# One inference step with 96 attention units and a paged decode: the order of the work of one unit step on TensorE

## The chip, the cores and the metric

The kernel runs on one core of one Trainium2 chip. The metric is the device time of one launch in microseconds (us), the median of several runs. Everything is computed in float32.

## What is computed

One layer of a hybrid decoder, for a prompt of 512 tokens and for 8 decode sequences of one new token each with 4096 cached tokens. Two attention branches run side by side: sparse attention (compressed, selected and sliding window keys) and latent attention (MLA). Both are gated, projected and added to the input:

```python
p_w = _masked_softmax(s_w, mask_w)                         # sliding window; the selected branch alike
o_w = einsum('bqgrs,bsgd->bqgrd', p_w, kvw[..., 1, :])
s = (einsum('bqhc,bsc->bhqs', q_lat, c) + einsum('bqhr,bsr->bhqs', q_pe, kr)) * MLA_SCALE   # c, kr: paged caches
o_lat = einsum('bqhs,bsc->bqhc', _masked_softmax(s, mask), c)
pa = (o_a * silu(ga)) @ w_proj_a
pb = (o_b * silu(gb)) @ w_proj_b
h = sigmoid(ma) * pa + sigmoid(mb) * pb                    # ga, gb, ma, mb = xn @ w_in (gate columns)
y = x + rmsnorm(h @ w_out, norm_post)
```

The page table says which pages of the caches belong to which sequence, so the latent cache (256 pages of 128 tokens, kept with its transpose, 256 KB a page) is loaded page by page.

## The kernel before

The kernel is written by hand for the five engines, each with its own instruction stream; they meet in semaphores. It has a first part (projection, compression and selection), a loop of 99 unit steps, and a tail (merge of the decode parts, the output projections, the norm). The change lies in the loop and in TensorE's stream alone.

**The loop.** Step u = 0..98 puts up to four streams of work beside each other on TensorE:

- *The prompt's units.* 96 units, each one head and one block of 128 queries against 128 to 512 keys. `scores(u)` (L889) runs on even u and writes the scores of units u and u+1 into two PSUM banks; it waits until ScalarE has taken the exponentials (L1236) of units u-2 and u-1. `transposes(u-2)` (L897) turns the probabilities; it waits until VectorE has scaled them and until the transposes of the unit before are copied out. `outputs` (L910) on even u multiplies units u-4 and u-3 with the values, after both copies.
- *The decode's chunks.* 80 steps from u = 2 on: `K` steps turn keys (`dec_keys`, L932), `C` steps treat one chunk c. `dec_scores(c)` (L950) needs the chunk's data in its ring slot, and waits until the exponentials of the chunk before it are taken (they free bank 5). VectorE then forms the maximum (L1775), ScalarE the exponential (L1253). One step later `dec_transposes(c)` (L920) turns the probabilities, VectorE or ScalarE copies them out, and `dec_outputs(c)` (L961) multiplies them with the values. Its last matmul raises `do_ps`.
- *The fills.* From u = 36 to 95 each step has a quarter of one column block of the gate projection, in four parts, `fill(u, 0)` to `fill(u, 3)`. Steps come in fives (x = 0..4): for x < 4 a part is one 128x512 gate product (L980), for x = 4 (u = 40, 45, 50, ..., 95) it is eight small products for the decode rows (L985). Bank 3 has to be read out after x = 1, 3 and 4, and the next fill waits for that reading (L1299 on ScalarE, L1291 and L1832 for the silu gates).

**The order in the other streams.** VectorE takes in a step: silu of the last fill, the copy of `dec_transposes` (every other chunk), `unit_max(u)` (L1728), the maximum of the chunk, the scaling of unit u-1, the copy of unit u-2, the reading of `outputs`, and `dec_fold` after `dec_outputs`. ScalarE takes: the reading of the last fill, its share of the copies, the exponentials of unit u, then those of the chunk, then its share of the unit copies. All are strictly in order, so a copy that waits holds up what is queued behind it.

**The MLA chunks and their loads.** Steps 42 to 81 hold eight groups of five: for each sequence a chunk "new" (the new token, no load) and four parts, each with its own load of 2 MB into a ring of three slots. The part steps of the first group are u = 43, 44, 45, 46, of the second 48, 49, 50, 51, and so on: the fourth part always meets x = 0, and the step before it x = 4. SyncE starts the eight page loads (L500) of job n as soon as the slot's last user, the chunk three loads earlier, has raised `do_ps`:

```python
            elif J_WIN <= m < J_WV:
                eng.wait_ge(S["do_ps"], last_chunk[m] + 1)        # slot_free, m = n - RING, RING = 3
```

The fourth part's slot is that of the first part of the same sequence, whose `dec_outputs` is in the step after its `dec_scores`. GpSimd fetches the rotary keys of the job (L537) after the same signal.

**The array's shapes.** The products use TensorE's array in four shapes: whole (128x128: `transposes`, `dec_transposes`, `dec_keys`, the L980 fills, and `scores` of the units 0 to 31 with 96 rows), four column strips (128x32: `dec_scores`, `dec_outputs`, the L985 fills), two column strips (128x64: `outputs`), and 64 rows (`scores` from unit 32 on).

Of the kernel before, what the change touches and what calls it, by code (L numbers as in the profile page):

```python
# [167 lines left out]
def build(nc, t):  # L168

    ctx = ExitStack()  # L170
    with ctx:
# [34 lines left out]
        def C(name, lo=0, width=None, rows=P):  # L206
            off, _, w = CST[name]
            return cst[0:rows, off + lo:off + (w if width is None else lo + width)]
# [111 lines left out]
        def job_landed(eng, n):  # L320

            eng.wait_ge(S[slot_sem(n)], landed[n])
# [3 lines left out]
        chunks = []  # L326
# [20 lines left out]
        UNITS = 96  # L347
# [16 lines left out]
        def dt_copied(eng, m):  # L364

            if m >= 0:
                eng.wait_ge(S["dt_by_" + dt_use[m]], sum(1 for e in dt_use[:m + 1] if e == dt_use[m]))
# [16 lines left out]
        def fill_free(eng, ev):  # L384

            if ev >= 0:
                def silu(e):
                    return FILL_JOBS[e // 3][0] in ("ga", "gb")
                eng.wait_ge(S["fill_by_dve" if silu(ev) else "fill_by_act"], sum(1 for e in range(ev + 1) if silu(e) == silu(ev)))
# [40 lines left out]
        def unit(u):  # L430

            if u < 32:
                return 2, 2 * (u // 8) + u % 2, (u % 8) // 2
            v = u - 32
            return (v % 4) // 2, 2 * (v // 16) + v % 2, (v % 16) // 4
# [7 lines left out]
        def pt_by(u):  # L443
            return "A" if u % 2 else "V"
# [141 lines left out]
        def K_of(c):  # L586
            r, part = c["r"], c["part"]
            out = []
            for j in range(4):
                if c["kind"] == "win":  # L590
                    q = QZw[:, (4 * r + j) * 32:(4 * r + j + 1) * 32]
                    out.append([(q, KnW if part == "new" else KTs[:, j * 512:(j + 1) * 512], 0, c["width"])])
                elif c["kind"] == "slc":
                    s2 = 0 if part == "new" else part
                    q = QZs[:, ((4 * r + j) * 2 + s2) * 32:((4 * r + j) * 2 + s2 + 1) * 32]
                    out.append([(q, KnS[:, (j % 2) * 8:(j % 2) * 8 + 8] if part == "new" else KTs[:, j * 512:(j + 1) * 512], 0, c["width"])])
                else:
                    ql = [QL[:, (ck * 8 + r) * 32:(ck * 8 + r + 1) * 32] for ck in range(2)]
                    qr = [QR[:, (r * 4 + v) * 32:(r * 4 + v + 1) * 32] for v in range(4)]
                    if part == "new":  # L600
                        out.append([(ql[0], cTn[:, 0:8], 0, 8), (ql[1], cTn[:, 8:16], 0, 8), (qr[0], krn, 0, 8)])
                    else:
                        pages = job(c["job"]).rearrange("p (q c) -> p q c", q=8)
                        kr = KRR[:, ((c["job"] - J_MLA) % RING) * 256:][:, 0:256]
                        row = [(ql[ck], pages[:, 2 * j:2 * j + 2, 256 + ck * P:256 + (ck + 1) * P], 0, 256) for ck in range(2)]
                        for q2 in range(2):
                            q = 2 * j + q2
                            row.append((qr[q % 4], kr[:, (q // 4) * P:(q // 4 + 1) * P], q2 * P, P))
                        out.append(row)
            return out  # L610
# [18 lines left out]
        def _(pe):  # L629
# [245 lines left out]
            def scores(u):  # L875

                if u >= 2:
                    pe.wait_ge(S["p"], u)
                for x in (u, u + 1):
                    br, h, tl = unit(x)  # L880
                    width = (tl + 1) * P
                    if br < 2:
                        e, g = h % 2, h // 4
                        q = qrT[64 * e:64 * e + 64, (h // 2) * 512 + tl * P:(h // 2) * 512 + (tl + 1) * P]
                        kk = KT2[64 * e:64 * e + 64, (br * 2 + g) * 512:(br * 2 + g) * 512 + width]
                    else:
                        q = qmT[0:96, h * 512 + tl * P:h * 512 + (tl + 1) * P]
                        kk = kmT[0:96, h * 512:h * 512 + width]
                    pe.matmul(bank[x % 2][:, 0:width], q, kk, start=True, stop=True).then_inc(S["s"], 1)  # L889

            def transposes(u):
                _, _, tl = unit(u)
                pe.wait_ge(S["p_scaled"], u + 1)
                if u >= 1:
                    pe.wait_ge(S["pt_by_" + pt_by(u - 1)], (u - 1) // 2 + 1)
                for kb in range(tl + 1):
                    mm = pe.transpose(bank[2][:, kb * P:(kb + 1) * P], Pb[u % 3][:, kb * P:(kb + 1) * P], ident)  # L897
                mm.then_inc(S["pt_ps"], 1)
# [36 lines left out]
            def dec_scores(c):  # L935
                if c["n"] >= 1:
                    pe.wait_ge(S["dp"], c["n"])
                if c["kind"] == "mla" and c["part"] != "new":
                    job_landed(pe, c["job"])
                    m = c["job"] - J_MLA  # L940
                    pe.wait_ge(S[f"kr{m % RING}_landed"], 32 * (m // RING + 1))
                if c["kind"] != "mla" and c["part"] != "new":

                    for j in (2, 3):
                        dt_copied(pe, use_of[("K", c["job"], j)])
                rows = K_of(c)
                for x in range(len(rows[0])):
                    for j in range(4):
                        q, kk, at, w = rows[j][x]
                        mm = pe.matmul(bank[5][32 * j:32 * j + 32, at:at + w], q, kk,  # L950
                                       start=(x == 0), stop=(x == len(rows[0]) - 1))
                mm.then_inc(S["ds"], 1)
# [12 lines left out]
            def fill(step, part):  # L965

                i = step - FILL_STEP
                if not 0 <= i < len(FILLS):
                    return
                x, n = FILLS[i][2], i // 5  # L970
                if part == 0:
                    if x in (0, 2, 4):
                        fill_free(pe, 3 * n + x // 2 - 1)
                    if i == 0:
                        pe.wait_ge(S["xg2"], KM)
                    if x == 0:
                        pe.wait_ge(S[f"gate_w{n % 2}"], 16 * (n // 2 + 1))
                if x < 4:
                    k, sub = 4 * (x % 2) + part, x // 2
                    mm = pe.matmul(bank[3][:, :], gate_w[n % 2][:, k * 256 + sub * P:k * 256 + (sub + 1) * P],  # L980
                                   XG[:, k * TOK:k * TOK + SEQ], start=(k == 0), stop=(k == KM - 1))
                else:
                    for k in (2 * part, 2 * part + 1):
                        for j in range(4):
                            mm = pe.matmul(bank[3][32 * j:32 * j + 32, 0:64], XG[:, k * TOK + SEQ:k * TOK + SEQ + 32],  # L985
                                           gate_w[n % 2][:, k * 256 + j * 64:k * 256 + (j + 1) * 64], start=(k == 0), stop=(k == KM - 1))
                if part == 3 and x in (1, 3, 4):
                    mm.then_inc(S["fill_ps"], 1)
# [3 lines left out]
            prev = None  # L992
            for u in range(UNITS + 3):
                st = steps[u - FIRST_STEP] if FIRST_STEP <= u < FIRST_STEP + len(steps) else None
                if prev is not None:
                    dec_transposes(prev)
                if u < UNITS and u % 2 == 0:
                    scores(u)
                fill(u, 0)
                if st is not None and st[0] == "K":  # L1000
                    dec_keys(st[1], st[2])
                if st is not None and st[0] == "C":
                    dec_scores(chunks[st[1]])
                fill(u, 1)
                if 2 <= u < UNITS + 2:
                    transposes(u - 2)
                fill(u, 2)
                if u >= 4 and u % 2 == 0:
                    outputs((u - 4) // 2)
                if prev is not None:  # L1010
                    dec_outputs(prev)
                fill(u, 3)
                prev = chunks[st[1]] if st is not None and st[0] == "C" else None


# [1095 lines left out]
```

## Time and profile before

| | |
|---|---|
| median of 3 runs (lowest to highest) | 928.52 us (927.67 to 929.01) |
| the profiled execution's own time | 938.05 us |
| its span, first to last instruction | 936.2 us |
| TensorE matmul busy | 819.7 us, 88% |
| VectorE, ScalarE, GpSimd busy | 359.8, 208.1, 112.0 us |
| mean granted TensorE clock | 0.948 |
| the loop of unit steps | about 271 to 798 us of the span |
| moved by DMA | 170.46 MB, mean 182 GB/s |

In the rows below a line of the timeline gives the start, the length, the engine, the kernel's line, the operation with its tiles and shape, and how many instructions are merged in it; in brackets stands how long the engine was idle before it and what ended that. A float32 matmul shows as two records. The length of a TensorE record includes the time that its last columns need to come out, so lengths of consecutive rows overlap; distances from start to start are the time that the work takes. A releaser "issue" is one that the profile can't name: the wait of `dec_scores` for its ring slot shows so.

### The profile page before, as it was taken

Reading aid. Unit: us, or ns where it says so; the run is one execution under the profiler, and the core shown is the slowest. Engines: PE = TensorE matmul, PEld = TensorE weight load, DVE = VectorE, ACT = ScalarE, POOL = GpSimd, SP = SyncE. Lnnn points to the kernel's source line nnn. Section 1 sums busy time; section 2 is a strip of 40 time slices with the busy share of each in tenths; the row PEclk is TensorE's granted clock in tenths of the full one; section 3 lists DMA queues with packets and bytes.
Section 4 is the critical chain, followed back from the end, with each engine's and each line's share of the span. In section 5 each row is a group of like instructions: output and inputs, shape, how many; then the busy total and the mean of one; then the engine's idle time right before and its main releaser. Section 6 shows DMA issues by size and latency. Waiting matters only on the chain.

```text
span 936.2 us, 16303 instructions
## 1 busy us (share of the span) xinstructions
PE 819.7 (88%) x6373; PEld 419.0 (45%) x6373; DVE 359.8 (38%) x1136; ACT 208.1 (22%) x599; POOL 112.0 (12%) x125
## 2 busy tenths in 40 slices
PE   6999997688967776899899799898999999999994
PEld 3444442474544443444443344443345444544442
DVE  2100002669256744544433334332454233332234
ACT  0400000521314333432221222222222222000111
POOL 0311220100011130000221122112120000000000
PEclk9999999769879887999999899998999999999998
DMA  8897566650072231622869659686596510040301
GB/s 333 348 419 296 202 267 250 236 184 1 15 257 91 91 99 32 213 82 91 295 237 324 237 200 350 215 285 236 192 343 222 206 46 1 1 180 1 137 23 47
DMA packets 59855, 170.46 MB, mean 182 GB/s; under 512 B 7466, under 2 KB 11715, under 8 KB 52995
## 3 DMA queue, kind: packets, MB, share of 16 engines
q1 hardware_dynamic: 48450, 108.46, 32.3%
q0 software_dynamic: 9600, 48.38, 13.7%
q10 hardware_dynamic: 1728, 12.58, 3.6%
q8 instruction: 51, 0.84, 0.4%
q14 instruction: 26, 0.21, 0.1%
HBM read 165.06 MB, written 8.52 MB: 185 GB/s over the span
## 4 chain that ended last, share of the span: by engine, by line
PE 83%; DVE 7%; issue 5%; ACT 3%; DMA 1%; another core or an unknown queue 1%; SPq 1%; ACTq 0%; DVEq 0%
PE bank L980 20%; PE bank L665 12%; PE bank L950 7%; PE bank L1097 6%; PE bank L1112 6%; PE bank L889 5%; PE bank L961 4%; PE bank L679 3%; PE bank L910 3%; PE bank L897 3%; PE bank L807 2%; PE bank L920 2%; PE bank L985 1%; PE bank L932 1%; PE bank L824 1%
## 5 line engine op out<-in xcount | busy, mean ns | idle before, releaser
L980 PE MATMUL bank<-XG,W 128*128 128x512 f32 x384 | 206.0, 630 | 7.2 <-DVE projD L1832 3.6
L665 PE MATMUL bank<-W,XG 128*128 128x494 f32 x256 | 109.7, 587 | 3.2 <-DMA W<-w_attn 3.2
L537 POOL DMA_INDIRECT KRR<-krT,idxi x64 | 60.4, 943 | 310.3 <-PE bank L961 299.7
L980 PEld LDWEIGHTS bank<-XG,W 128*128 128x128 f32 x384 | 60.0, 191 | 59.1 <-issue 44.0
L1236 ACT ACTIVATE projP<-bank,W 128x128 f32<-128x128 f32 (+3 forms) x96 | 50.4, 525 | 149.7 <-DVE W L1728 141.0
L665 PEld LDWEIGHTS bank<-W,XG 128*128 128x128 f32 x256 | 48.6, 192 | 61.9 <-issue 61.4
L889 PE MATMUL bank<-W 64*128 64x128 f32 (+7 forms) x192 | 53.0, 507 | 17.3 <-ACT projP L1236 10.6
L1728 DVE CUSTOM_DVE_ANT_0 bank<-bank,maskb 128x128 f32<-128x128 f32 (+3 forms) x96 | 47.5, 495 | 49.2 <-PE bank L889 47.7
L1775 DVE TENSOR_REDUCE sm<-bank 128x1 f32<-128x256 f32 (+2 forms) x56 | 22.8, 408 | 87.1 <-PE bank L950 86.3
L950 PE MATMUL bank<-ring,W 128*32 128x256 f32 x512 | 36.6, 406 | 19.4 <-issue 19.4
L897 PE MATMUL bank<-cst,projP 128*128 128x128 f32 x240 | 45.3, 288 | 7.6 <-DVE projP L1736 7.1
L897 PEld LDWEIGHTS bank<-cst,projP 128*128 128x128 f32 x240 | 30.7, 146 | 40.7 <-issue 38.8
L537 POOL DMA_INDIRECT ring<-cmp,idxi x32 | 30.0, 938 | 119.2 <-PE bank L679 91.1
L1112 PE MATMUL bank<-ring,W 128*128 128x512 f32 x96 | 42.5, 592 | 0.0
L961 PE MATMUL bank<-ring,W 128*32 128x256 f32 (+2 forms) x832 | 42.0, 330 | 0.0
L1131 ACT ACTIVATE W<-bank 64x512 f32<-64x512 f32 (+3 forms) x56 | 26.9, 483 | 63.2 <-PE bank L920 31.6
L889 PEld LDWEIGHTS bank<-W 64*128 64x128 f32 (+1 forms) x192 | 22.6, 202 | 35.6 <-issue 15.0
L1812 DVE SCALAR_TENSOR_TENSOR projP<-projP,sm,bank 128x256 f32<-128x256 f32 (+2 forms) x42 | 18.3, 436 | 51.3 <-PE bank L961 51.3
L679 PE MATMUL bank<-ring,cst 128*32 128x256 f32 x512 | 32.1, 407 | 5.8 <-issue 5.8
L1356 DVE TENSOR_SCALAR projP<-bank,sm 128x494 f32<-128x494 f32 x8 | 5.9, 732 | 78.9 <-PE bank L665 78.8
L950 PEld LDWEIGHTS bank<-ring,W 128*32 128x32 f32 x512 | 14.8, 113 | 43.8 <-issue 39.1
L1250 ACT ACTIVATE sm<-sm 128x1 f32<-128x1 f32 x42 | 12.4, 295 | 92.6 <-DVE sm L1779 92.4
(337 smaller groups left out, 1086.3 us busy)
## 6 DMA issues: line engine op xcount, KB each, us to landing
ring<-latent SPq DMA_DIRECT2D x256, 256.0 KB
W<-w_gate ACTq DMA_DIRECT2D x12, 1024.0 KB, 7.7
W<-w_attn SPq DMA_DIRECT2D x16, 494.0 KB, 8.9
ring<-win SPq DMA_DIRECT2D x8, 512.0 KB
ring<-w_out SPq DMA_DIRECT2D x2, 2048.0 KB
o_win<-win SPq DMA_DIRECT2D x1, 4088.0 KB
XG<-xT SPq DMA_DIRECT2D x4, 520.0 KB, 8.4
XG<-xT SPq DMA_DIRECT2D x1, 2080.0 KB, 8.0
```

Of the source, the lines that this page charges most:

```text
L537: pool.indirect_dma_start(out=dst, out_offset=None, in_=src, in_offset=bass.IndirectOffsetOnAxis(ap=idxi[:, col:col + 1], axis=0)).then_in ...
L665: mm = pe.matmul(bank[2 * (u % 2) + n][:, 0:GW], XG[:, k * TOK + tl * P:k * TOK + (tl + 1) * P], W[:, w:w + GW], start=(k == 0), stop=(k = ...
L679: mm = pe.matmul(bank[5 + b % 2][32 * i:32 * i + 32, 0:256], C("pool"), src, start=(r == 0), stop=(r == 7))
L889: pe.matmul(bank[x % 2][:, 0:width], q, kk, start=True, stop=True).then_inc(S["s"], 1)
L897: mm = pe.transpose(bank[2][:, kb * P:(kb + 1) * P], Pb[u % 3][:, kb * P:(kb + 1) * P], ident)
L950: mm = pe.matmul(bank[5][32 * j:32 * j + 32, at:at + w], q, kk, start=(x == 0), stop=(x == len(rows[0]) - 1))
L961: mm = pe.matmul(bank[7][32 * j:32 * j + 32, 0:c["pv"]], PTd[0:k, blk * P + 32 * j:blk * P + 32 * j + 32], V_of(c, blk, j), start=(blk == ...
L980: mm = pe.matmul(bank[3][:, :], gate_w[n % 2][:, k * 256 + sub * P:k * 256 + (sub + 1) * P], XG[:, k * TOK:k * TOK + SEQ], start=(k == 0), ...
L1097: mm = pe.matmul(bk[:, :], w[:, x * P:(x + 1) * P], (OB if ab else OA)[:, k * 512:(k + 1) * 512], start=(k == 0), stop=(k == 3))
L1112: mm = pe.matmul(bk[:, :], MB[k][:, x * P:(x + 1) * P], w, start=(k == 0), stop=(k == KM - 1))
L1236: act.activation(Pb[u % 3][:, 0:w], bank[u % 2][:, 0:w], ACT.Exp, bias=NMp[:, u:u + 1], scale=-1.0, accum_out=RSp[:, u:u + 1]).then_inc(S[ ...
L1728: dve.tensor_tensor_reduce(bank[u % 2][:, 0:w], bank[u % 2][:, 0:w], maskb[:, 512 - w:512], -1.0, 1e38, ALU.add, ALU.min, NMp[:, u:u + 1]) ...
```

## The change

The order of the calls in one unit step of TensorE's stream. Before: decode transposes of the last chunk, unit scores, fill part 0, decode keys or decode scores, part 1, unit transposes, part 2, unit outputs, decode outputs, part 3. After: decode scores, unit scores, unit transposes, decode transposes, decode keys, the four fill parts in one run, unit outputs, decode outputs. No instruction is added or removed, every wait stays with its call, and the streams of the other engines are as they were.

```diff
             for u in range(UNITS + 3):
                 st = steps[u - FIRST_STEP] if FIRST_STEP <= u < FIRST_STEP + len(steps) else None
+                if st is not None and st[0] == "C":
+                    dec_scores(chunks[st[1]])
+                if u < UNITS and u % 2 == 0:
+                    scores(u)
+                if 2 <= u < UNITS + 2:
+                    transposes(u - 2)
                 if prev is not None:
                     dec_transposes(prev)
-                if u < UNITS and u % 2 == 0:
-                    scores(u)
-                fill(u, 0)
                 if st is not None and st[0] == "K":
                     dec_keys(st[1], st[2])
-                if st is not None and st[0] == "C":
-                    dec_scores(chunks[st[1]])
-                fill(u, 1)
-                if 2 <= u < UNITS + 2:
-                    transposes(u - 2)
-                fill(u, 2)
+                for part in range(4):
+                    fill(u, part)
                 if u >= 4 and u % 2 == 0:
                     outputs((u - 4) // 2)
                 if prev is not None:
                     dec_outputs(prev)
-                fill(u, 3)
                 prev = chunks[st[1]] if st is not None and st[0] == "C" else None
```

## Rows read from the trace of the kernel before

**Rows 1.** Windows by stage, TensorE: length, busy, clock, DMA share, GB/s.

```profile
271.00:391.00 120.00, 88.64 (x837) 0.86 0.32 110
391.00:422.00 31.00, 29.66 (x226) 1.00 0.31 103
422.00:730.20 308.20, 279.97 (x3048) 0.97 0.70 247
730.20:797.80 67.60, 63.45 (x464) 1.00 0.21 78
```

**Rows 2.** Waits of TensorE: line, releaser, us in total, times, longest.

```profile
PE bank L950 <- issue: 19.4, 8, 4.7
PE bank L889 <- ACT projP L1236: 10.6, 8, 2.6
PE bank L920 <- ACT projP L1253: 9.8, 9, 2.1
```

**Rows 3.** Groups of TensorE's instructions: busy, mean ns, idle before them, its releasers.

```profile
L980 PE MATMUL bank<-XG,W 128*128 128x512 f32 x384 | 206.0, 630 | 7.2 <-DVE projD L1832 3.6 <-ACT W L1299 1.3 <-issue 0.7
...
L985 PE MATMUL bank<-W,XG 128*32 128x64 f32 x768 | 19.3, 222 | 6.0 <-DVE projD L1832 3.6 <-ACT W L1299 1.6 <-ACT projP L1299 0.7
```

**Rows 4.** Timeline of TensorE, steps 44 to 46.

```profile
443.90 1.07 PE L961 MATMUL bank<-ring,W 128*32 128x256 f32 x16
444.90 1.13 PE L980 MATMUL bank<-XG,W 128*128 128x512 f32 x2
445.86 0.38 PE L920 MATMUL bank<-cst,projP 128*128 128x128 f32 x2
447.43 0.43 PE L985 MATMUL bank<-W,XG 128*32 128x64 f32 x16 [1.19 <-DVE projD L1832]
447.68 1.05 PE L950 MATMUL bank<-ring,W 128*32 128x256 f32 x16
...
449.32 0.55 PE L897 MATMUL bank<-cst,projP 128*128 128x128 f32 x3
...
450.05 1.05 PE L961 MATMUL bank<-ring,W 128*32 128x256 f32 x16
...
451.61 1.13 PE L889 MATMUL bank<-W 64*128 64x512 f32 x4
452.67 1.12 PE L980 MATMUL bank<-XG,W 128*128 128x512 f32 x2
456.00 1.07 PE L950 MATMUL bank<-ring,W 128*32 128x256 f32 x16 [2.20 <-issue]
```

**Rows 5.** Timeline of TensorE, two gate products in a run, step 82.

```profile
730.83 1.99 PE L980 MATMUL bank<-XG,W 128*128 128x512 f32 x4
732.65 0.27 PE L897 MATMUL bank<-cst,projP 128*128 128x128 f32 x1
```

**Rows 6.** Timeline of SyncE's queue, one load of 2 MB.

```profile
525.24 5.09 SPq L500 DMA_DIRECT2D ring<-latent  x8
```

**Rows 7.** Timeline of TensorE, steps 54 and 56, the longest wait.

```profile
518.12 1.07 PE L961 MATMUL bank<-ring,W 128*32 128x256 f32 x16
...
531.65 1.94 PE L950 MATMUL bank<-ring,W 128*32 128x256 f32 x16 [4.67 <-issue]
533.33 1.11 PE L950 MATMUL bank<-KRR,projP 128*32 128x128 f32 x16
```

**Rows 8.** Timeline of TensorE, steps 79 and 81, the last load.

```profile
712.74 1.07 PE L961 MATMUL bank<-ring,W 128*32 128x256 f32 x16
...
724.34 1.07 PE L950 MATMUL bank<-ring,W 128*32 128x256 f32 x16 [1.09 <-issue]
```

**Rows 9.** Timeline of TensorE, step 34, before the fills begin.

```profile
383.97 0.63 PE L920 MATMUL bank<-cst,projP 128*128 128x128 f32 x4 [1.42 <-ACT projP L1253]
384.53 0.49 PE L889 MATMUL bank<-W 64*128 64x128 f32 x4
384.95 1.06 PE L950 MATMUL bank<-projP 128*32 128x512 f32 x8
```

## The prediction, made before the result was known

> **What bounds the kernel now.** I read the windows by stage first, then TensorE's waits, then the timeline of one group of five steps. TensorE is the engine of the whole span, and the change touches only the loop, which has four stretches [rows 1]: steps 0 to 35 without fills (120 us, TensorE busy for 88.6 of them), 36 to 41 (31 us), the MLA steps 42 to 81 (308.2 us, busy 280) and 82 to 98 (67.6 us). In the MLA stretch the DMA engines are busy for 0.70 of the time at 247 GB/s, far above the other stretches. The waits say where TensorE is late there: `dec_scores` waits 8 times, 19.4 us in all, for something that the profile can't name [rows 2]. The eight are the fourth parts of the eight sequences, and what they wait for is their ring slot: in the timeline the first part's `dec_outputs` (L961) ends at 443.90 + 1.07 = 444.97, and `dec_scores` of the fourth part starts at 456.00, after 2.20 idle [rows 4]. SyncE issues for 5.09 us for such a load [rows 6]. From the release to the start the eight cases take 11.03, 10.55, 12.46, 9.49, 10.47, 12.07, 9.81 and 10.53 us (the first, the third and the last are in [rows 4, 7, 8]), mean 10.8. I call that the turnaround; every other load has a step more in hand and is never waited for. So in this stretch TensorE's own work and the turnaround of one slot take turns as the bound. In the steps before the fills it is the chain over VectorE and ScalarE: 10.6 us at `scores` and 9.8 us at `dec_transposes` [rows 2].
>
> **Part 1: fewer changes of the array's shape (gain).** A gate product of 512 columns takes (732.65 - 730.83) / 2 = 0.91 us with the change of shape ahead of the pair in it, so about 0.86 alone [rows 5]. Behind four-strip work the same product takes 445.86 - 444.90 = 0.96, so 0.10 more; 16 strip products of 256 columns in four strips stream as long as one gate product, 0.86, and take 444.90 - 443.90 = 1.00 behind `outputs`, 0.14 more; 64-row scores of four times 512 columns, two rows at a time, stream 0.86 and take 452.67 - 451.61 = 1.06, 0.20 more [rows 4]. Where the shape stays nothing is added: `dec_scores` starts 0.25 behind a decode fill of the same strips (447.43 to 447.68) [rows 4]. Now I count through the 99 steps: the old order changes shape 361 times, the new one 245 times; of the 116 that go, 96 are in the MLA steps, where `dec_outputs` of one step and `dec_scores` of the next now follow each other in one shape and the fills no longer cut in. At 0.16 each (between 0.10 and 0.20, nearer the upper end since most of those that go lead back into a gate product or into scores) that is 18.6 us; bounds 11.6 and 23.
>
> **Part 2: the fills wait less for bank 3 (gain).** Behind x = 1, 3 and 4 a fill begins the next step at once and waits for ScalarE or VectorE to read bank 3: 7.2 us at L980 and 6.0 us at L985 in the whole loop [rows 3]. In the new order outputs, decode outputs, scores and transposes stand between the last part and the next first one, 1.5 to 4 us, longer than such a wait (1.19 in [rows 4]). I take 11 of the 13.2 us; bounds 5 and 13. What may be late instead is `dec_outputs`, which waits for the copy of `dec_transposes`: four gate products (3.4 us) cover it, four decode parts (1.0 us) hardly.
>
> **Part 3: the window of the fourth load shrinks (loss).** The fourth part's slot is released at the end of `dec_outputs` in step x = 3. Before, until the fourth part wants it, TensorE still has part 3 of that step, all of step x = 4, and transposes, scores and part 0 of step x = 0: 456.00 - 2.20 - 444.97 = 8.83 us [rows 4]. In the new order `dec_outputs` is the last call of a step and `dec_scores` the first, so only step x = 4 is left, the short one: `dec_scores` 1.30, transposes 0.45, decode transposes 0.22, the four decode parts 1.1, `dec_outputs` 0.88, together 3.95 us when the step is odd (from the distances in [rows 4], with 0.25 for a decode part); on even steps scores and outputs of 0.2 to 0.9 each with their changes of shape make it 5.5. The turnaround starts at the same release and isn't shortened. Waits: 4 x (10.8 - 3.95) + 4 x (10.8 - 5.5) = 27.4 + 21.2 = 48.6 us against 19.4 now, a loss of 29.2. Everything on TensorE is queued behind this wait, the unit scores and all four fills, and with them the two engines that read them. The other loads keep two whole steps. The shortest two are x = 1 and 2: with 3.5 for four gate products, 1.3 for one full `dec_scores`, 0.9 and 0.45 for two `dec_outputs`, 1.5 for transposes of both kinds and 1.5 to 2 for the one scores and the one outputs that fall in them, they come to 12.5 to 13 us (prices from [rows 4, 5]), against a turnaround of 10.8 on the mean and 12.5 at most: covered, with little to spare. Bounds of the term: with the shortest turnaround of the eight (9.5) 19, with the longest (12.5) 43.
>
> **Part 4: the clock falls in each of these waits (loss).** The granted clock of the MLA stretch is 0.97 [rows 1], which is about 18 us at 1.2 GHz instead of 2.4. It belongs to the three longest waits: behind the one of 4.67 us `dec_scores` takes 1.94 instead of 1.07 [rows 4, 7]; the waits of 2.2 us left the clock alone [rows 4]. So three spells of some 6 us, part of each in the wait itself; I put what is lost at 2.3 us a spell, between 0.87 (that one row) and 3. With waits of 5.3 and 6.9 us all eight fall: 5 more spells, 11.5 us; bounds 4 and 15. The Trainium skill has the same pattern as a rule (TensorE: Matmul & The Clock Gate, "HAM oscillation — how this bites in real kernels"): a wait for a transfer in every round of a loop lets the clock drop each time, and the next burst starts slow. By that rule, too, the order that gathers eight longer waits pays for each.
>
> **Part 5: the steps without fills (loss, small).** With two chunks in a row the chain from `dec_transposes` to its copy, then `unit_max` and the unit's exponentials now starts behind `dec_scores`, scores and transposes. At step 34 decode transposes come at 383.97, scores at 384.53, decode scores at 384.95 and take 1.00 [rows 9]; after the change the wait of 1.42 stays (it is the same semaphore), the scores come about 1 us later and the copy 1.5 to 2 us later. Three such steps (20, 27, 34), 5 us; in the other chunk steps `dec_outputs` now waits 0.5 to 0.9 us for its copy, for the larger part inside waits of [rows 2] that exist anyway; earlier transposes and ten fewer changes of shape (counted above) give a little back. I take 6 us; bounds 0 and 12. The K steps only swap transposes and keys: nothing.
>
> **Sum.** -18.6 - 11 + 29.2 + 11.5 + 6 = +17.1 us. On the profiled execution's own span of 936.2 that is 953.3, of its time of 938.05 it is 955.2. The profiled execution is 9.5 us longer than the median of the runs, 928.5; the terms are the same on either, so the median should be 945.5.
>
> **Rivals.** (a) *The switches win; on the other side.* If the turnaround were not tied to the release, the fourth part would wait no longer than now, and parts 3 and 4 fall away: 928.5 - 18.6 - 11 + 6 = 905. The turnaround decides: each microsecond less of it takes 8 us from part 3 and below 9 the clock stays up as well, so from about 8.8 us on the kernel is faster. For it speaks that nearly two thirds of the turnaround are SyncE's issuing and the transfer, which may run more freely when TensorE stands still; against it that the shortest of eight is 9.5 and that bytes and queue are the same. The Trainium skill's page TensorEngine Tiling (Array Packing), "Key Properties", says that changing the tiling mode drains TensorE; the trace agrees, with 0.10 to 0.20 us for a change [rows 4]. By that rule alone the time would be 928.5 - 18.6 = 910, and this rival is its case. (b) *The loss is larger.* The other loads have little to spare: if the second and third parts, too, wait (a turnaround of 12.5 or more against 12.5 to 13), or the gate weights' loads, now nearer to the fourth load, slow it, some 1 to 2 us in each group come on top, 8 to 16 us: 960. (c) *It evens out.* Turnaround 9.5, clock lost half as often, nothing in part 5: -18.6 - 11 + 19 + 6 + 0 = -5 to 0: no change. That the change doesn't do what it says can't be: the order of TensorE's stream is the order of the calls.
>
> **How the numbers follow.** Forecast (parts 3 and 4 as sized, 932 to 955) 0.74; (b) 0.12; (c) 0.04, within 0.2% of the old time, about what a measurement can tell from no change; (a) 0.10. The time is that of the forecast, 945. The range 930 to 961 leaves out (a) and the ends of the others, about 2 in 10. Slower 0.85, same 0.03, faster 0.12 (rival (a), and the part of (c) below the old time).
>
> **What would show it.** In the profile after: L950's idle "issue" near 49 us in 8 waits of 4 to 9 us, all in steps x = 0; the clock of the MLA stretch near 0.93; L980 and L985 idle below 3 us; the stretch 82 to 98 shorter by 3 to 4 us; the stretch before the fills longer by some 6. Wrong it would be if the eight waits stay near 2.5 us each (the turnaround gave way), or if `dec_outputs` or `scores` in the fill steps show waits of their own above 5 us in all, which I have costed at the 2 us left out of part 2.

## The result, and the profile after

| | before | after |
|---|---|---|
| median of 4 runs each, side by side | 928.76 us | 963.13 us (956.95 to 967.76) |
| ratio | | 1.036, 95% interval 1.030 to 1.043 |
| the profiled execution's own time | 938.05 us | 961.75 us |
| its span | 936.2 us | 960.0 us |
| mean granted clock | 0.948 | 0.919 |

The change costs 34 us. The forecast was 945, slower by 16.5: the sign held, the size was half, and the time lies above the range of 930 to 961.

The waits of TensorE (line, releaser, us in total, times, longest), which answer to [rows 2]:

```profile
PE bank L950 <- DMA ring<-latent: 71.8, 8, 9.8
```

The eight waits for the fourth part's ring slot have gone from 19.4 us to 71.8, and the profile can now name what they wait for, the load. The forecast was 49. The windows by stage (length, TensorE busy, clock, DMA share, GB/s), as in [rows 1]:

```profile
270.60:383.80 113.20, 86.85 (x835) 0.89 0.34 116
...
414.10:758.50 344.40, 272.58 (x3066) 0.89 0.64 221
758.50:821.30 62.80, 61.14 (x466) 1.00 0.23 84
```

All of the loss is in the MLA steps, 308.2 to 344.4 us; the steps behind them gained 4.8 us. The steps before the fills are 6.8 us shorter, but the profile before holds one stall of 7.07 us there that none of the forecast's terms contains (first experiment below). The groups of the two kinds of fills, as in [rows 3] (busy, mean ns, idle before them):

```profile
L980 PE MATMUL bank<-XG,W 128*128 128x512 f32 x384 | 175.7, 601 | 0.0
...
L985 PE MATMUL bank<-W,XG 128*32 128x64 f32 x768 | 13.2, 221 | 0.1
```

Both are without idle time, where they had 7.2 and 6.0 us: the second gain that was forecast is there. And the first wait of the eight, which answers to [rows 4] (timeline of all engines, steps 44 to 46):

```profile
434.15 1.07 PE L961 MATMUL bank<-ring,W 128*32 128x256 f32 x16
...
435.98 9.12 SPq L500 DMA_DIRECT2D ring<-latent  x16
...
437.15 1.10 PE L985 MATMUL bank<-W,XG 128*32 128x64 f32 x64
...
438.44 0.33 ACTq L1273 DMA_DIRECT2D W<-w_gate  x1
448.40 1.94 PE L950 MATMUL bank<-ring,W 128*32 128x256 f32 x16 [9.28 <-DMA ring<-latent]
```

The slot is released at 434.15 + 1.07 = 435.22. TensorE reaches the wait at 448.40 - 9.28 = 439.12, 3.90 later: the window is what was predicted (3.95). But `dec_scores` starts only at 448.40, 13.18 after the release and not 10.8. In between stands a line that the forecast gave only to a rival: at 438.44, 3.2 after the release, ScalarE issues the load of the gate weights (1 MB). Before it came later:

```profile
451.39 0.34 ACTq L1275 DMA_DIRECT2D W<-w_gate  x1
```

That is 6.4 after the release at 444.97 [rows 4]. ScalarE issues it once the last fills that read the old weights are done, the decode fills of x = 4. In the new order these four parts stand in one run early in the step, and the load moved forward with them.

### The profile page after: what moved, and what is told of

It is laid out like the page before. It is cut to its first block, busy times and chain, and to the rows that moved or that the text cites. A ratio compares the mean times of both kernels' runs of the same rounds, so it can differ in the third digit from the quotient of the medians.

```text
span 960.0 us, 16303 instructions
## 1 busy us (share of the span) xinstructions
PE 809.2 (84%) x6373; PEld 430.4 (45%) x6373; DVE 351.0 (37%) x1136; ACT 201.4 (21%) x599; POOL 112.6 (12%) x125
## 2 busy tenths in 40 slices
DMA packets 59854, 170.46 MB, mean 178 GB/s; under 512 B 7465, under 2 KB 11714, under 8 KB 52994
## 4 chain that ended last, share of the span: by engine, by line
PE 75%; DMA 8%; DVE 8%; issue 3%; SPq 3%; ACT 2%; ACTq 0%; DVEq 0%
PE bank L980 17%; PE bank L665 11%; DMA ring<-latent 8%; PE bank L1095 6%; PE bank L1110 6%; PE bank L950 6%; PE bank L889 5%; PE bank L961 4%; PE bank L897 3%; PE bank L679 3%; PE bank L910 3%; SPq L500 2%; PE bank L920 1%; PE bank L932 1%; PE bank L807 1%
## 5 line engine op out<-in xcount | busy, mean ns | idle before, releaser
L980 PE MATMUL bank<-XG,W 128*128 128x512 f32 x384 | 175.7, 601 | 0.0
L980 PEld LDWEIGHTS bank<-XG,W 128*128 128x128 f32 x384 | 70.9, 195 | 71.0 <-issue 70.6
L950 PE MATMUL bank<-ring,W 128*32 128x256 f32 x512 | 40.8, 444 | 71.8 <-DMA ring<-latent 71.8
L537 POOL DMA_INDIRECT KRR<-krT,idxi x64 | 60.9, 952 | 333.8 <-PE bank L961 323.1
L665 PEld LDWEIGHTS bank<-W,XG 128*128 128x128 f32 x256 | 48.6, 192 | 61.5 <-issue 61.0
L950 PEld LDWEIGHTS bank<-ring,W 128*32 128x32 f32 x512 | 17.1, 122 | 88.6 <-issue 81.9
L897 PE MATMUL bank<-cst,projP 128*128 128x128 f32 x240 | 49.7, 307 | 5.4 <-DVE projP L1734 1.8
L1795 DVE COPY W<-bank 128x256 f32<-128x256 f32 (+2 forms) x28 | 12.6, 451 | 97.8 <-PE bank L920 97.8
L897 PEld LDWEIGHTS bank<-cst,projP 128*128 128x128 f32 x240 | 28.1, 148 | 39.0 <-issue 33.2
L537 POOL DMA_INDIRECT ring<-cmp,idxi x32 | 30.0, 938 | 118.8 <-PE bank L679 91.1
L889 PEld LDWEIGHTS bank<-W 64*128 64x128 f32 (+1 forms) x192 | 22.6, 208 | 35.1 <-issue 15.6
```

The lines of the kernel that those rows point to most:

```text
L537: pool.indirect_dma_start(out=dst, out_offset=None, in_=src, in_offset=bass.IndirectOffsetOnAxis(ap=idxi[:, col:col + 1], axis=0)).then_in ...
L665: mm = pe.matmul(bank[2 * (u % 2) + n][:, 0:GW], XG[:, k * TOK + tl * P:k * TOK + (tl + 1) * P], W[:, w:w + GW], start=(k == 0), stop=(k = ...
```

## Where the time of the MLA steps went

From the records of TensorE I took for each call when its columns stream, and for each gap what ended it. A gap is counted here from the last column streamed, which makes a wait up to 0.2 us longer than the idle time in a profile row. Steps 42 to 81, in us:

| kernel | length | columns streaming | gaps under 0.25 | fourth-part waits | other waits |
|---|---|---|---|---|---|
| before | 308.1 | 241.5 | 33.0 | 19.7 | 13.9 |
| after | 344.3 | 252.9 | 18.5 | 71.9 | 0.9 |

The differences: fewer changes of shape -14.5, fills no longer waiting -13.0, eight waits +52.2, slower clock +11.4, together +36. Over the kernels that are shown below, this is the turnaround of the fourth part's slot (release to start of `dec_scores`, mean of eight) against when the gate weights' load is issued:

| kernel | gate load, us after the release | turnaround | eight waits |
|---|---|---|---|
| before | 5.6 to 7.7 | 10.8 | 20 |
| after | 3.0 to 4.7 | 13.6 | 72 |
| e1_gate_later | not in this time | 10.8 | 49 |
| e2_next_later | 3.0 to 4.7 | 13.3 | 69 |
| e3_both_later | not in this time | 10.7 | 48 |
| e5_run_only | 4.0 to 4.5 | 13.7 | 60 |
| e6_scores_first_only | 5.4 to 7.5 | 11.0 | 39 |
| e4_scores_late (in three of the eight nothing is waited for) | 5.6 to 5.8 | 12.1 | 10 |
| e10_late_from_36 | 4.1 to 5.6 | 13.8 | 31 |
| e11_late_and_gate | not in this time | 10.8 | 8 |

## Experiments

Kernels that ran side by side share the runs of the kernel before; from group to group that one's median differs (928, 942 and 929, on three chips), so the ratios are what is compared.

**Base.** The kernel before once more.

> The kernel before once more, for a second profile of it. The first profiled execution took 9.5 us more than the median, and it held one wait of 7.1 us at the unit transposes of step 25 that no order explains. If that stall belongs to the one execution, this profile has none there and a time near 929 us; if it belongs to the kernel, it stands here too and the time is near 938.

Its profiled execution took 936.2 us, the waits 19.1 us in 8, the turnaround 10.75. Steps 2 to 35 took 106.9 us and not 116.0: the first profiled execution had one stall of 7.07 us there, which is not in this one.

```profile
355.89 1.09 PE L897 MATMUL bank<-cst,projP 128*128 128x128 f32 x4 [7.07 <-DVE projP L1736]
```

It comes and goes with the execution, and the forecast's base contains it. A stall of 5.1 or 7.1 us at this place stands in four of the eight traces whose first 36 steps have the order before or nearly so (before, e5_run_only, e6_scores_first_only, e7_pair_at_end) and in none of the five with the order after. These are too few to say whether the order has a part in it.

**Which load lengthens the turnaround?** Theory G: the gate weights' load. Theory N: the next latent load, which SyncE issues right behind.

e1_gate_later, from the changed kernel:

```diff
-                if x == TILES and i // 5 + 2 < len(FILL_JOBS):
-                    gate_load(i // 5 + 2)
+                if x == 1 and 2 <= i // 5 + 1 < len(FILL_JOBS):
+                    gate_load(i // 5 + 1)
```

> The changed kernel, with the reload of the gate weights issued behind x = 1 of the next column block instead of behind x = 4, so two steps later, out of the way of the fourth part's load. Theory G: the turnaround of the fourth load grew because the gate weights' 1 MB, which now starts about 3.5 us behind the release instead of 6.6, shares the DMA engines with it. Then the turnaround falls back to about 11 us, the eight waits to about 50 us from 71.8, and the time to about 943. Theory N: it grew because the next load of the same queue now follows directly behind it. Then the turnaround stays near 13.4, the waits near 72, the time near 963.

e2_next_later:

```diff
                 slot_free(sp, n)
+                if n > J_MLA and (n - J_MLA) % 4 == 0:
+                    sp.wait_ge(S[slot_sem(n - 1)], landed[n - 1])
```

> The changed kernel, with one wait more on SyncE: the first part's load of the next sequence is issued only when the fourth part's load has landed. Theory G: nothing changes, turnaround near 13.4, waits near 72 us, time near 963. Theory N: the turnaround falls to about 11, the waits to about 50, the time to about 943.

e3_both_later has both edits.

> The changed kernel with both delays. Theory G: as with the gate weights later alone, about 943. Theory N: as with the next load later alone, about 943. If each has a part, this is faster than either alone and the turnaround is that of a load that runs by itself, about 10 us.

Measured: 948.4 (ratio 1.019, 1.009 to 1.030), 960.5 (1.031, 1.022 to 1.041) and 949.6 (1.019, 1.010 to 1.028). TensorE's waits of e1_gate_later:

```profile
PE bank L950 <- DMA ring<-latent: 49.3, 8, 7.8
PE bank L950 <- issue: 7.8, 6, 1.9
```

and of e2_next_later (its lines stand two further down, L952 is `dec_scores`):

```profile
PE bank L952 <- DMA ring<-latent: 68.8, 8, 9.4
```

With the gate load away the turnaround is 10.8 again and the eight waits are 49.3 us, against 48.6 in the forecast; holding the next latent load back takes 3 us. G holds, N falls. The first run also shows what moves elsewhere: the gate load now starts 4.1 to 5.5 us after the slots of the second parts are free, and `dec_scores` waits for them, 7.8 us in all. By the landings in the trace these loads take 12.8 to 14.6 us there, and 9.5 to 10.5 in after, where no gate load meets them. That is the same effect on another load. The Trainium skill says that loads issued by different engines "will ultimately run on the same 16 DMA engines and interleave with each other" (DMA: Bandwidth & Descriptors, "Issuing engines are not separate DMA queues"). The runs agree; what it costs shows only in them: next to nothing when the 1 MB starts some 6.5 us after the release (before, e6), 2.8 us when it starts 3.0 to 4.7 after (after).

**Which half of the change does it?** Each from the kernel before; the lists are the calls of one step.

```diff
-DT S F0 K DS F1 T F2 O DO F3      (before)
+DT S K DS T F0 F1 F2 F3 O DO      (e5_run_only)
+DS DT S F0 K F1 T F2 O DO F3      (e6_scores_first_only)
+S T DT K F0 F1 F2 F3 DS O DO      (e4_scores_late)
```

Here DS is decode scores, DT and T the transposes, S and O scores and outputs, DO decode outputs, K keys, F0 to F3 the fill parts.

> Before's order with the fills alone gathered: decode transposes, unit scores, decode keys or scores, unit transposes, four fill parts, outputs, decode outputs. Decode outputs are last of the step as in the change, decode scores come a little later than there. Window of the fourth load 0.4 to 1.4 us longer than in the changed kernel, turnaround as there (13.4), so the eight waits sum to about 63 us; ten changes of shape in two steps against six. Time about 962. If decode scores at the head were the whole cause, it would be near before's 928 or under it.

> Before's order with decode scores alone moved to the head of the step; fill part 3 still follows decode outputs. Window of the fourth load about 1 us longer than in the changed kernel, the gate weights' load about 1 us later, turnaround about 12 us: eight waits of 50 us in all against 20 of before, all eight with a fall of the clock, plus 10, and no change of shape saved. Time about 968. If gathering the fills were the whole cause, it would be near 928.

> The changed kernel with one call moved: decode scores behind the four fill parts instead of at the head of the step, ahead of the outputs. Theory G (the window of the fourth load and the clock carry the loss): the window grows by transposes and four gate products, 4 to 5 us, so the eight waits fall from 72 to about 34 us and the clock loses less, minus 40 us; against that one change of shape more in two steps and the decode chain less well covered, plus 5 to 12. Time about 935. If the loss came instead from moving the fills or the outputs, it stays near 963.

Measured against 942.15 before: e5 971.7 (1.031, 1.029 to 1.033), e6 950.6 (1.010, 1.006 to 1.014), e4 920.3 (0.975, 0.970 to 0.979). The expectations of e6 and e4 were missed: against a kernel before of 928 they said 1.04 and 1.007. The run of four fills alone brings nearly the whole loss: it takes two fill parts out of the window behind the release and brings the gate load forward, and its wait is

```profile
456.00 1.94 PE L950 MATMUL bank<-ring,W 128*32 128x256 f32 x16 [6.60 <-DMA ring<-latent]
```

Decode scores first alone has a short window but not the early gate load, and I had put it at 968, with a turnaround of 12 and waits of 50 us: it kept 11.0, with waits of 39. The same run of fills *with* the decode scores behind it beats both kernels: a whole run of gate products now lies between release and need, and the eight waits are 10 us where I had expected 34.

**Is the order alone a gain, when the load is no bound?** Each page load moves 128 of 512 columns. The other three quarters of the bytes are left out, and the latent branch computes on old data there.

```diff
-sp.dma_start(job(n)[:, q * 512:(q + 1) * 512], ...rearrange("a p n -> (a p) n"))
+sp.dma_start(job(n)[:, q * 512:q * 512 + 128], ...rearrange("a p n -> (a p) n")[:, 0:128])
```

> The kernel before, with one change: each page load of the latent cache moves only the first 128 of its 512 columns, so that three quarters of those bytes are left out and the latent branch works on old data in the rest. All instructions stay. It is the base for the run of the changed kernel with the same cut. The turnaround of the slot should fall from 10.9 to about 7 us (eight issues of 0.52 us stay), below the window of 8.8 us, so the eight waits (19 us) go, and with them the three spells at half clock (some 7 us): about 902 where the uncut kernel takes 928, ratio 0.972.

> The changed kernel with the same cut: each latent page load moves only 128 of 512 columns; three quarters of the bytes are left out and the latent branch works on old data in the rest. What the order itself gains should now show without the load. Theory (fewer changes of shape 15 us, bank 3 read in time 13 us, both in the MLA steps, and 5 us in the steps behind them): turnaround about 7 us against windows of 3.95 and 5.5, so waits of 1.5 to 3 us stay, some 18 us in all, mostly too short to drop the clock; against the cut kernel before 15 to 25 us less: about 882, ratio 0.95 to before. Rival (the gain exists only because TensorE stood still so long that the other engines caught up): once the long waits are gone, waits for ScalarE and VectorE come back at the fills or the outputs, over 8 us in all in the MLA steps, and the time is 895 or more.

Measured: 906.3 for the order before (ratio 0.976, 0.971 to 0.981) and 934.7 for the order after (1.008, 1.005 to 1.011). My expectation of 882 for the second was wrong: the turnaround fell to 9.6 us only, not to 7, and the eight waits stayed at 39.6 us.

```profile
PE bank L950 <- DMA ring<-latent: 24.0, 4, 6.2
PE bank L950 <- issue: 15.6, 4, 5.5
```

These loads still have the gate load beside them. In e9_before_quarter, where it starts 5.6 to 7.7 us after the release, `dec_scores` waits for one of the eight alone, 3.6 us. From the landings in the trace, the last bytes of the cut load are there 7.5 us after the release on the mean of the eight (seven at 6.2 to 7.8, one at 11.1), against 10.7 for the whole load in before; in e8_after_quarter it is 9.5, against 13.5 in after. So three quarters of the bytes are worth 3 to 4 us in either order, and the 7 us that I had expected came out in one order alone; between the two orders, and so with the early gate load, even a quarter of the bytes takes 2 us more. With 40 us of waits left, this pair does not show the order alone. For the same reason it leaves the rival open, that other engines take over once the waits are gone; no other wait shows in the profile of the MLA steps.

**The combination.** e7_pair_at_end keeps the old order up to step 35; from 36 on a step is S F0 F1 T DT K F2 F3 O DO DS, which puts decode outputs and decode scores side by side at the end and leaves a window of nearly two steps.

> An order made from the theory: from step 36 on unit scores, two fill parts, both transposes, two fill parts, outputs, decode outputs and decode scores side by side at the end; before step 36 before's order. As few changes of shape as in the change, but a window of nearly two steps, 10.7 to 12.5 us, for the fourth load. Theory G: the eight waits sum to about 16 us, the clock stays up, the gain of fewer shape changes (15 us) and of the fills' waits (11 us) is kept, minus some 8 us where decode transposes now wait for the exponentials. Time about 905. If the gain of fewer changes of shape isn't real, it is no faster than 925.

It took 1003.8 (1.067, 1.064 to 1.070), by far the slowest, where I had expected 905. The window did what was said: none of the eight loads is waited for. Its groups of fills:

```profile
L980 PE MATMUL bank<-XG,W 128*128 128x512 f32 x384 | 196.9, 638 | 46.8 <-DVE projD L1848 20.7
...
L985 PE MATMUL bank<-W,XG 128*32 128x64 f32 x768 | 21.4, 273 | 33.6 <-ACT W L1315 18.0
```

80 us of waiting for bank 3 where before had 13. The timeline behind step 44 shows why:

```profile
450.72 0.62 PE L950 MATMUL bank<-KRR,projP 128*32 128x128 f32 x16
...
453.20 0.42 DVE L1791 TENSOR_REDUCE sm<-bank 128x1 f32<-128x256 f32 x1 [5.57 <-remote]
...
455.31 0.68 DVE L1848 SCALAR_TENSOR_TENSOR projD<-projD,bank 128x512 f32<-128x512 f32 x1
...
456.04 1.08 PE L985 MATMUL bank<-W,XG 128*32 128x64 f32 x32 [4.70 <-DVE projD L1848]
```

The reading of bank 3 (L1848) stands in VectorE's stream behind the maximum of the chunk (L1791), and that waits for decode scores, now the last call of the step. The next step begins with fills and finds the bank unread. The maximum is also late by itself, 1.9 us after the last matmul it needs (450.72 + 0.62), of which more in the last section. I had costed window and switches and had not followed the in-order streams of VectorE and ScalarE.

e10_late_from_36 has the old order up to step 35 and the order of e4_scores_late from 36 on; e11_late_and_gate is the same with the edit of e1_gate_later.

> The order before in steps 0 to 35, which have no fills; from step 36 on: scores, transposes, decode transposes, keys, four fills in a run, decode scores, outputs, decode outputs. The run with that order in all steps had 291 us in the MLA steps against 310 before, 63.5 against 67.5 in steps 82 to 98, but 121 against 107 in steps 2 to 35. If the loss there belongs to the order and not to the chip, this one is at 928 - 18 - 4 = 906, ratio 0.973 to 0.96. If steps 2 to 35 stay at 115 or more (a stall that comes with the chip), it is at the earlier run's ratio of 0.975.

> The same with the gate weights' load moved behind x = 1 of the next block. In the run with this order two of the eight turnarounds were 14.8 us and those two waits 4.1 and 3.7 us (steps 71, 76), 10.3 in all. If it is the gate weights' load that makes them long, the eight waits fall to 3 us or less and the time is 5 to 7 us below the run without it: about 900. If the second parts' loads then wait, as they did with the changed order (6 waits of about 1.9 us in dec_scores at x = 3), half or all of that is given back: 902 to 908.

Measured: e10 929.8 (0.999, 0.996 to 1.003), e11 **899.0** (0.969, 0.964 to 0.974), the fastest here. The two differ in the gate load alone, so moving it out of the way is worth 31 us in this order, the strongest evidence for theory G. e10 was expected at 906, since e4 had gained 18 us in the MLA steps. Its steps 2 to 35 are back at 106.9 us (121.3 in e4), so the loss there did belong to the order; but the eight waits are 31 us and not 10. (Each trace is of the slowest execution of its kernel, 936.1 us of ten for e10 and 927.0 of four for e4.)

```profile
PE bank L950 <- issue: 30.4, 8, 4.8
```

From step 36 on the calls are the same. What differs in e4's trace is ten idle spells of up to 0.5 us in the decode fills, 4.2 us in all, which the profile can't name. They delay the gate load from 4.1 to 5.6 us after the release to 5.6 to 5.8, and the turnaround was 12.1 and not 13.8: six of the eight took 10.8 to 11.6 us, two 14.6. Between 5.4 and 5.8 us the time of the gate load does not settle the turnaround: in e4 it is 14.6 behind a gate load at 5.65 and 11.5 behind one at 5.70, in before 12.5 behind one at 5.6 and 10.5 behind one at 5.8, in e10 13.7 behind one at 5.56. What decides there is open, and so is why the spells are in the one kernel and not in the other. With the gate load out of the way, e11 has, in the same order:

```profile
413.00:692.50 279.50, 258.21 (x3054) 1.00 0.78 272
```

MLA steps of 279.5 us at full clock (308.2 at 0.97 in [rows 1]), the eight waits together 7.7 us, none over 1.4. About 900 was expected, but as 5 to 7 us less than a run without the edit at 906; against the 929.8 of e10 it is 31.

## Why the prediction was wrong in size

**Part 1 (changes of shape, -18.6).** Right. The gaps under 0.25 us fell by 14.5 in the MLA steps (96 of the 116 changes, forecast 15.4) and by 3.0 in the rest of the loop, 17.5 in all. The traces, counted, have 361 changes of shape (second execution of before) and 244.

**Part 2 (bank 3, -11).** Right in the mechanism, a little small: 13.1 us of L980 and L985 are gone, and `dec_outputs`, which might have been late instead, has no wait in the profile from step 36 on.

**Part 3 (the fourth load, +29.2).** The step that failed, and only in one of its two numbers. The windows were 3.8 to 4.0 on odd steps and 4.9 to 5.9 on even ones, as said. The turnaround, taken as unchanged because "the turnaround starts at the same release and isn't shortened", was not the load's own: it grew from 10.8 to 13.6 because the change moved another load into it. Eight times 2.83 is 22.6 of the 23 us that this term lacks (52.2 against 29.2). The sum followed what the new order lets SyncE issue and when; it did not ask what else is issued behind the calls that move: the last reading of the fills lets ScalarE issue the gate weights, and the fills had moved forward. Rival (b) named that load, at 1 to 2 us a group, with a time of 960 and a chance of 0.12; it had the mechanism and came nearest to the 963, with a price that was too small. e1_gate_later, where the turnaround is 10.8 again, came out at 948.4, 3 us from the forecast's 945.5, its eight waits at 49.3 us (forecast 48.6). Its new waits of 7.8 us are in that time and in no term, so the closeness is in part luck.

**Part 4 (clock, +11.5).** Right: streaming took 11.4 us more, all eight waits were followed by half the clock. e11_late_and_gate, with none of these spells, streams the same steps in 235.1 us, so the eight cost (252.9 - 235.1) / 8 = 2.2 each, where 2.3 was put.

**Part 5 (steps without fills, +6).** Too high. Steps 2 to 35 took 109.1 us, against 106.9 in the second execution of before and 108.9 in the first without its stall: +2.2 or +0.2, and 1.5 more with the gain in changes of shape set apart. New waits do stand behind the three steps named, 1.84 us at unit transposes of step 21, 1.68 at decode scores of 27, 1.39 at unit transposes of 35, but those of `dec_transposes` ahead of them (2.31, 0.91 and 1.62 us at 20, 27 and 34 in the second execution of before) went or shrank: the waits moved more than they grew.

**From the profile to the median.** The sum was made on a profiled execution 9.5 us above the median, with the remark that the terms are the same on either. After's profiled execution is 1.4 us below its median. On profiled executions the forecast, 955.2, misses 961.75 by 6.6; on medians it misses by 17.6. Of these 11 us, 7.1 are the stall of the profile before, which after's profile has not: with it taken off the base the miss is 13.6, so the 6.6 is half luck. That does not close the matter, since e0_before_again, without the stall, was still 7.9 us above the median of its group; its first part is 2.2 us and its tail 3.3 us longer than in the first profile. What makes the kernel before, and not after, slower in the profiled execution stays open.

**Rivals.** (a), the switches win, was wrong for this order. e4 and e11, with fills in a run and a longer window, come to ratios of 0.975 and 0.969, that is 905 and 900 on a kernel before of 928.5; but they also gain 10 to 12 us of the eight waits and raise the clock of the MLA steps from 0.97 to 0.99 and 1.00, which are not in (a)'s sum. That its 905 lies near them does not confirm it. (c) did not happen: the turnaround never came near 9.5.

## What to carry to other kernels

When a block of work moves in one engine's stream, list what its *last* instruction permits elsewhere: a buffer's refill moves with it, and may land on top of the one transfer that is on the critical path. A turnaround read from the trace is a measurement of that load among its present neighbours, not a property of the load. A run of same-shaped work did best here (e4, e11) between a release and the need for what it frees; and before calls go to the end of a step, follow the in-order streams that wait for them.

## What the runs showed of the hardware

- A load of 2 MB in eight issues by SyncE is ready 10.7 to 10.8 us after its slot is free on the mean of eight, 9.8 to 11.7 each, when no gate load starts in that time (e1, e3, e11). A 1 MB load from ScalarE's queue that starts 3 to 5 us after the release adds 2.5 to 3 us, one that starts later than 5.8 us mostly nothing, and between 5.4 and 5.8 both are seen (table above).
- With a quarter of the bytes in as many packets (59,854 against 59,855 in the whole run) the same load is there after 7.5 us in the mean (e9_before_quarter), and after 9.5 us with the early gate load beside it (e8_after_quarter), against 10.7 and 13.5 with all bytes.
- In e7_pair_at_end VectorE is idle and waiting for decode scores in all 32 chunks that have a latent load. In 22 of them its maximum starts 1.6 to 1.9 us after the last matmul, as at 453.20 above, with nothing named but "remote". In exactly these 22 GpSimd issues its two gathers (L537) around that moment, since decode outputs, which release them, stand right ahead of decode scores, and the maximum starts 1.5 to 1.6 us after the start of the second. In the other 10 no gather runs and it starts after 0.07 us, as in all 32 such chunks of before (0.04 to 0.07). 22 times 1.8 is 40 us. No run moved the gathers alone, so it is a correlation, and they can't be the whole cause: in after, four chunks (508.65 us and three more) have the gathers at the same distances, the last matmul being 1.0 us behind the first and 0.25 ahead of the second, and there the maximum starts after 0.07 us. VectorE had then been idle for 0.6 us at most, against over 5 in the 22:

```profile
508.65 0.42 DVE L1773 TENSOR_REDUCE sm<-bank 128x1 f32<-128x256 f32 x1 [0.42 <-PE bank L950]
```

- The length of a wait does not settle the clock behind it. In the second execution of before (timeline of TensorE) a wait of 2.33 us is followed by half the clock, 1.94 us for 16 matmuls, and one of 2.50 us by the full one, 1.07:

```profile
565.36 1.94 PE L950 MATMUL bank<-ring,W 128*32 128x256 f32 x16 [2.33 <-issue]
...
642.58 1.07 PE L950 MATMUL bank<-ring,W 128*32 128x256 f32 x16 [2.50 <-issue]
```
